# High-part products ahead of low-part products in the first projection behind each norm of a two-block fp32 kernel

## The chip, the cores and the metric

The kernel runs on one core of one Trainium2 chip. The metric is device time in microseconds for one execution. The kernel before took 1255.28 us, the median of three runs (1248.02 to 1257.01).

## The reference, cut to what matters

Two transformer blocks in a row on one sequence of 512 tokens, width 1024, everything in fp32. The first block has two layers; each has an attention mixer and a gated embedding stage behind it ("ple"):

```
for i in range(2):
    h = rms_norm(x, norm_g[i])
    x = x + mixer_i(h)                 # neighbourhood attention, then GQA with rotary
    g = sigmoid(rms_norm(x, ple_norm_g[i]) @ ple_w_gate[i])
    x = x + g * (p[i] @ ple_w_proj[i])
x = rms_norm(x, final_norm_g)
```

The second block is one layer: `h = rms_norm_2(x, norm_g_2)`, a wide input projection `h @ w_in_2`, a sparse attention mixer and a recurrent mixer (RWKV-7) side by side, an output projection, and a last norm. So there are five norms that are followed by a projection: norm0, ple0, norm1, ple1 and norm2.

## The kernel before, in words

**Split products.** TensorE is fed with fp32 numbers that are split in two rounded parts, high and low. A product of activations and weights is made of three: high x high, high activations x low weights, low activations x high weights. `three` (line 498 on) issues them for one k, `tm3` for one tile of 128 tokens and 256 output columns (24 products: 8 values of k times 3), `fm3` for 128 output features and all 512 tokens (24 products of 512 columns). All of them accumulate in one PSUM bank.

**How parts come about.** For weights (a half is 1024 x 256 numbers, in the ring of buffers): SyncE loads them, ScalarE copies the high part (`high`, line 1308), POOL subtracts and leaves the low part in place, in four pieces (`lower`, line 2503). `need3` lets TensorE wait for the fourth piece of a half. For activations behind a norm, in tiles of 128 tokens: VectorE computes the norm and scales a tile (line 1792, semaphore `xn_`), TensorE transposes it (`turn`, two halves of four blocks), VectorE multiplies with the gain out of the bank (`gain_half`, line 1804, or 1801 at norm2), ScalarE copies the high part (`high_half`, line 1313, semaphore `hi_`), and the low part is made by POOL for tiles 0 to 2 (`low_half`, line 2509, semaphore `lo_`) and by VectorE for tile 3 (line 1815, semaphore `lo3_`). A half (hf 0 or 1) holds k = 0 to 3 or 4 to 7.

**Order behind a norm.** Each engine has its own program, written out by hand. TensorE, at the end of the stage ahead, runs `tail`: three tiles, the turn of tile 0, the fourth tile, the turn of tile 1. Then `head`: for tile i the 24 products of block 0 (with the six products of the embedding projection behind them in ple0 and ple1), and behind tiles 0 and 1 the turns of tiles 2 and 3. `head` serves ple0, ple1 and norm1. ScalarE's `head` (line 1319 on) copies the high parts of tile 1, drains tile 0's bank, copies tile 2, then copies the high part of the next weights, drains tile 1, copies tile 3, drains the rest. VectorE's `ple` adds tile 0's result, does the gain of tile 2, adds tile 1's, does the gain of tile 3 and its low parts. POOL makes the low parts of tiles 0 to 2 ahead of those of the next weights.

**norm2** has its own order (lines 758 to 782): all eight transposes, for half 0 of the four tiles and then for half 1; then two `fm3` of 512 tokens with the weights Ckv (banks kvc 0 and 1). POOL makes three of the eight low halves, VectorE five. Behind Ckv come Csel, Cq 0 and others.

The waits sit in front of the products: in `head`, `ready(k)` waits at k = 0 and k = 4 for the low half of the tile, although the first two products of each k read high parts only. At norm0 the same is written out at line 611; that place is not in the diff.

Of the kernel before, what the change touches and what calls it, by code (L numbers as in the profile page):

```python
# [33 lines left out]
P = 128  # L34
# [3 lines left out]
KB = D // P  # L38
# [68 lines left out]
def program(nc, A, out):  # L107
    ctx = ExitStack()
    with ctx:
# [13 lines left out]
        def sem(name):  # L123
            return ctx.enter_context(nc.semaphore(name))
# [41 lines left out]
        for name, src in (("norm0", A["norm_g"][0:1]), ("norm1", A["norm_g"][1:2]),  # L166
# [6 lines left out]
            n = src.shape[1] // P  # L173
# [56 lines left out]
        for part in range(2):  # L230
            for n in range(2):
                w = A["w_out_2"][0][512 * part:512 * part + 512, 512 * n:512 * n + 512]
                load(("CO", part, n), w.rearrange("(k p) n -> p k n", p=P), (4, 512), False)

        def raw_slot(n):
            return ring[:, HALF * (n % NRAW):HALF * (n % NRAW) + HALF]

        def high_slot(n):
            o = HALF * (NRAW + splits.index(n) % NHI)
            return ring[:, o:o + HALF]  # L240
# [18 lines left out]
        def parts(high, low, k):  # L259

            return tuple(rounded(v.rearrange("p (k m) -> p k m", k=k)) for v in (high, low))

        def W3(name):
            n = HI[name]
            k, m = halves[n][1]
            return parts(high_slot(n)[:, 0:k * m], raw_slot(n)[:, 0:k * m], k)
# [25 lines left out]
        def S(name):  # L292

            if name not in made:
                made[name] = sem(name)
            return made[name]
# [17 lines left out]
        def evacuated(eng, key):  # L314

            eng.wait_ge(drained[who[key]], nth[key])
# [128 lines left out]
        def _(pe):  # L445
            def begin(key, consumer, apart=False):

                n = len(order)
                if n >= NBANK:
                    evacuated(pe, order[n - NBANK])  # L450
                order.append(key)
                if not apart:
                    opened.append(key)
                slot[key], who[key] = n % NBANK, consumer
                return bank[slot[key]]
# [3 lines left out]
            def end(ins, key=None):  # L459

                key = key or opened.pop(0)
                J[key] = len(J)
                count[who[key]] += 1
                nth[key] = count[who[key]]
                ins.then_inc(filled, 1)

            def mm(o, l, r, start, stop):
                return nc.tensor.matmul(o, l, r, start=start, stop=stop)  # L468
# [12 lines left out]
            def turn(tag, i):  # L481

                pe.wait_ge(S("xn_" + tag), i + 1)
                for hf in range(2):
                    turn_half(tag, i, hf, xn[:, i % 2, :])

            def need3(name):
                pe.wait_ge(s_wlo, 4 * splits.index(HI[name]) + 4)
# [4 lines left out]
            def three(o, left, right, start, stop):  # L493

                mm(o, left[0], right[0], start, False)
                mm(o, left[0], right[1], False, False)
                return mm(o, left[1], right[0], False, stop)

            def fm3(key, consumer, name, c0, act, ready=None, read=None):

                b = begin(key, consumer)
                w = W3(name)
                for k in range(KB):
                    if ready:
                        ready(k)
                    ins = three(b[:, :], [v[:, k, c0:c0 + P] for v in w], [v[:, k, :] for v in act], k == 0, k == KB - 1)
                    if read and k % 2 and k < KB - 1:
                        ins.then_inc(S(read), 1)
                end(ins)

            def tm3(key, consumer, w, i, c0, act, nk=KB, ready=None, m=256):

                b = begin(key, consumer)
                for k in range(nk):
                    if ready:
                        ready(k)
                    ins = three(b[:, 0:m], [v[:, k, i * P:(i + 1) * P] for v in act], [v[:, k, c0:c0 + m] for v in w],
                                k == 0, k == nk - 1)
                end(ins)
# [6 lines left out]
                jobs(3)  # L526
                turn(tag, 1)

            def head(tag, jobs):

                for i in range(NT):
                    def ready(k):
                        if k % 4 == 0 and i < 3:
                            pe.wait_ge(S("lo_" + tag), 2 * i + k // 4 + 1)
                        elif k % 4 == 0:
                            pe.wait_ge(S("lo3_" + tag), k // 4 + 1)

                    jobs(i, ready)
                    if i < 2:
                        turn(tag, i + 2)  # L540

# [29 lines left out]
            def ple(l, after):  # L571
                act = act3(f"ple{l}")
                pw = parts(pw_hi, pw_lo, 2)
                pT = tuple(rounded(v[:, :, :]) for v in (p_T, p_lo))
                for n in range(4):
                    need3(("PG", l, n))
                    if n == 0:
                        evacuated(pe, ("pT", l, 1))
                        pe.wait_ge(S("pw_low"), l + 1)

                    def jobs(i, ready=None):
                        tm3(("PG", l, n, i), "a", W3(("PG", l, n)), i, 0, act, ready=ready)
                        tm3(("PP", l, n, i), "v", pw, i, 256 * n, pT, nk=2)

                    if n == 0:
                        head(f"ple{l}", jobs)
                    elif n == 3 and after:
                        tail(jobs, after)
                    else:
                        for i in range(NT):  # L590
                            jobs(i)
                    used3(("PG", l, n))
# [5 lines left out]
            b = begin("vec", "a")  # L598
# [5 lines left out]
            act = act3("norm0")  # L604
            for n in AORD:
                need3(("A", n))
                if n == AORD[0]:
                    for i in range(NT):
                        def ready(k):
                            if k % 4 == 0:  # L610
                                pe.wait_ge(S("lo_norm0"), 2 * i + k // 4 + 1)
# [83 lines left out]
            act = act3("norm1")  # L695
            for n in range(10):
                need3(("B", n))
                if n == 0:
                    head("norm1", lambda i, ready: tm3(("B", 0, i), "a", W3(("B", 0)), i, 0, act, ready=ready))
                elif n < 6:  # L700
                    for i in range(NT):
                        tm3(("B", n, i), "a", W3(("B", n)), i, 0, act)
                else:
                    for s in range(2):
                        fm3(("B", n, s), "v", ("B", n), s * P, act)
                used3(("B", n))
            for i in range(NT):
                pe.wait_ge(S("B_rope"), i + 1)
                pe.wait_ge(S("B_rope_k"), i + 1)
                for hf in range(2):  # L710
                    b = begin(("BqT", i, hf), "a")
                    for q in range(4):
                        o = (4 * hf + q) * P
                        ins = nc.tensor.transpose(b[:, q * P:(q + 1) * P], qB[:, i, o:o + P], ident)
                    end(ins)
                b = begin(("BkT", i), "a")
                for g in range(4):
                    ins = nc.tensor.transpose(b[:, g * P:(g + 1) * P], kD[:, i, g * P:(g + 1) * P], ident)
# [44 lines left out]
                    pe.wait_ge(S("xn_norm2"), i + 1)  # L763
                    turn_half("norm2", i, hf, xn4[:, i, :])

            def ready2(k):

                if k % 4 == 0:
                    pe.wait_ge(S("lo_norm2"), (2, 3)[k // 4])
                    pe.wait_ge(S("lo3_norm2"), (2, 5)[k // 4])  # L770

            act2 = act3("norm2")
            need3("Ckv")
            for n in range(2):
                fm3(("kvc", n), "v", "Ckv", n * P, act2, ready2 if n == 0 else None)
            used3("Ckv")

            def tokens(name, key):
# [15 lines left out]
            b = begin("hid", "v", apart=True)  # L794
            for ii in range(16):
                for n, name in enumerate(("W1K", "W1V")):
                    if ii % 8 == 0:
                        need((name, ii // 8))
                    ins = mm(b[64 * n:64 * n + 64, 0:256], fl[:, n, ii * 64:ii * 64 + 64], W((name, ii // 8))[:, ii % 8, :],
                             ii == 0, ii == 15)  # L800
# [13 lines left out]
            for i in range(NT):  # L814
                for name, src in (("qp", q2), ("qr", q2r)):
                    b = begin((name, i), "a")
                    for j in range(4):
                        ins = nc.tensor.transpose(b[:, j * P:(j + 1) * P], src[:, i, j * P:(j + 1) * P], ident)
                    end(ins)
                b = begin(("kz", i), "a")  # L820
                for m in range(4):
                    ins = nc.tensor.transpose(b[:, m * P:(m + 1) * P], kd[:, i, m // 2, (m % 2) * P:(m % 2) * P + P], ident)
                end(ins)
            evacuated(pe, "hid")
            b = begin("hidT", "a")
            for m in range(2):
                ins = nc.tensor.transpose(b[:, m * P:m * P + P], hid_t[:, m * P:m * P + P], ident)
# [28 lines left out]
            b = begin("kcmp", "v")  # L856
            for blk in range(2):
                ins = mm(b[0:64, 0:64], w2[:, 0, blk, :], hid[:, 0, blk * 64:blk * 64 + 64], blk == 0, blk == 1)
            end(ins)
            b = begin("vcmp", "v")  # L860
            for g in range(2):
                for blk in range(2):
                    ins = mm(b[0:32, g * 64:g * 64 + 64], hid[:, 1, blk * 64 + g * 32:blk * 64 + g * 32 + 32],
                             w2[:, 1, blk, :], blk == 0, blk == 1)
# [100 lines left out]
            for j in range(4):  # L965
                bs = [begin((key, j), "a") for key in ("W", "A_")]
# [1726 lines left out]
```

## Time and profile before

| | us |
|---|---|
| median of 3 runs | 1255.28 (1248.02 to 1257.01) |
| the profiled execution, time | 1253.56 |
| the profiled execution, span | 1251.8 |
| TensorE busy | 1152.9 (92%) |
| VectorE busy | 596.9 (48%) |
| ScalarE busy | 509.6 (41%) |
| POOL busy | 450.4 (36%) |
| mean granted TensorE clock | 0.975 of full |

Busy times are sums over the whole span, and the stages differ. The stretches with the changed code are short: ple0 from 313 to 334 us of the span, norm1 from 379 to 397, ple1 from 653 to 675, norm2 from 729 to 753. A matmul row of the timeline shows start and duration; matmuls overlap, so the time that one takes from another's start to its own is shorter than its duration. In brackets stands how long the engine was idle ahead of the row, and what released it. The granted clock is given as a share of 2.4 GHz; its other level is 1.2 GHz, shown as 0.50.

### The profile page before, as it was taken

Reading aid. Unit: us, or ns where it says so; the run is one execution under the profiler, and the core shown is the slowest. Engines: PE = TensorE matmul, PEld = TensorE weight load, DVE = VectorE, ACT = ScalarE, POOL = GpSimd, SP = SyncE. Lnnn points to the kernel's source line nnn. Section 1 sums busy time; section 2 is a strip of 40 time slices with the busy share of each in tenths; the row PEclk is TensorE's granted clock in tenths of the full one; section 3 lists DMA queues with packets and bytes.
Section 4 is the critical chain, followed back from the end, with each engine's and each line's share of the span. In section 5 each row is a group of like instructions: output and inputs, shape, how many; then the busy total and the mean of one; then the engine's idle time right before and its main releaser. Section 6 shows DMA issues by size and latency. Waiting matters only on the chain.

```text
span 1251.8 us, 24943 instructions
## 1 busy us (share of the span) xinstructions
PE 1152.9 (92%) x10379; PEld 967.8 (77%) x10379; DVE 596.9 (48%) x1377; ACT 509.6 (41%) x1038; POOL 450.4 (36%) x391
## 2 busy tenths in 40 slices
PE   3999999999998999899999959988998889999996
PEld 3988887899898998566889949876776777777862
DVE  5000004733637169788245381137845755345546
ACT  4222224942324432888332353155854321133221
POOL 5744475873636445101544345130025460000000
PEclk9999999999999999999999979999999898999998
DMA  7433343332122332000331222431012222100001
GB/s 208 140 102 101 101 119 96 73 88 68 68 68 68 102 101 75 27 2 2 102 102 35 71 98 85 142 112 35 2 35 68 68 67 75 55 28 3 3 2 67
DMA packets 73178, 89.60 MB, mean 72 GB/s; under 512 B 1993, under 2 KB 66634, under 8 KB 72938
## 3 DMA queue, kind: packets, MB, share of 16 engines
q1 hardware_dynamic: 70136, 78.65, 19.5%
q0 software_dynamic: 2416, 8.26, 2.6%
q8 instruction: 82, 1.34, 0.4%
q10 hardware_dynamic: 514, 1.11, 0.4%
q14 instruction: 30, 0.25, 0.1%
HBM read 83.75 MB, written 4.26 MB: 70 GB/s over the span
## 4 chain that ended last, share of the span: by engine, by line
PE 73%; DVE 8%; issue 6%; POOL 5%; ACT 5%; DMA 2%; ACTq 0%; DVEq 0%; POOLq 0%
PE bank L468 68%; POOL ring_parts L2503 3%; PE bank L736 2%; ACT arena L1279 2%; DMA x<-x_kept 1%; DVE stat L1781 1%; PE bank L646 1%; PE bank L904 1%; ACT arena L1395 1%; DVE stat L1782 1%; POOL arena L2625 1%; DVE arena L1804 1%; DVE arena L1792 1%; ACT ring_parts L1308 1%; DVE x L1801 1%
## 5 line engine op out<-in xcount | busy, mean ns | idle before, releaser
L2503 POOL TENSOR_TENSOR ring_parts<-ring,ring_parts 128x512 fp32r<-128x512 f32 (+1 forms) x236 | 306.2, 1330 | 395.1 <-ACT ring_parts L1308 304.7
L468 PE MATMUL bank<-ring_parts,hT_parts 128*128 128x256 f32 x1664 | 329.2, 284 | 12.6 <-POOL arena_parts L2509 7.8
L468 PE MATMUL bank<-hT_parts,ring_parts 128*128 128x512 f32 x896 | 290.1, 402 | 15.7 <-POOL ring_parts L2503 10.0
L468 PEld LDWEIGHTS bank<-ring_parts,hT_parts 128*128 128x128 f32 x1664 | 267.9, 191 | 15.3 <-issue 11.1
L1279 ACT ACTIVATE arena<-bank 128x512 f32<-128x512 f32 (+3 forms) x356 | 166.9, 529 | 272.6 <-PE bank L468 264.2
L468 PE MATMUL bank<-ring_parts,arena_parts 128*128 128x256 f32 x1088 | 255.7, 284 | 3.4 <-POOL hT_parts L2520 3.4
L468 PE MATMUL bank<-arena 64*64 64x64 f32 (+6 forms) x3440 | 218.6, 276 | 9.3 <-ACT arena L1632 2.9
L468 PEld LDWEIGHTS bank<-hT_parts,ring_parts 128*128 128x128 f32 x896 | 173.1, 193 | 58.4 <-POOL ring_parts L2503 8.5
L468 PEld LDWEIGHTS bank<-arena 64*64 64x64 f32 (+2 forms) x3440 | 157.5, 141 | 62.7 <-issue 24.5
L468 PEld LDWEIGHTS bank<-ring_parts,arena_parts 128*128 128x128 f32 x1088 | 188.9, 190 | 4.3 <-POOL hT_parts L2520 3.8
L1308 ACT ACTIVATE ring_parts<-ring 128x2048 fp32r<-128x2048 f32 (+1 forms) x59 | 111.2, 1886 | 79.5 <-PE bank L468 79.4
L468 PE MATMUL bank<-arena_parts,ring_parts 128*128 128x512 f32 x256 | 101.1, 395 | 0.0
L1856 DVE SCALAR_TENSOR_TENSOR arena<-arena,bank 128x512 f32<-128x512 f32 x8 | 5.5, 688 | 172.0 <-ACT arena L1383 172.0
L468 PE MATMUL bank<-x_parts,ring_parts 128*128 128x512 f32 x192 | 78.7, 410 | 0.0
L468 PEld LDWEIGHTS bank<-arena_parts,ring_parts 128*128 128x128 f32 x256 | 48.0, 188 | 10.8
L2520 POOL TENSOR_TENSOR hT_parts<-hT,arena_parts 128x512 fp32r<-128x512 f32 x16 | 20.4, 1281 | 90.7 <-ACT arena_parts L1334 90.6
L2509 POOL TENSOR_TENSOR arena_parts<-arena,hT_parts 128x512 fp32r<-128x512 f32 x26 | 34.4, 1349 | 43.8 <-ACT hT_parts L1313 43.8
L468 PE MATMUL bank<-ring,arena 64*64 64x64 f32 (+3 forms) x512 | 49.2, 303 | 0.8 <-DMA ring<-in_cmp_w_v 0.7
L1509 ACT ACTIVATE arena<-bank,stat 128x512 f32<-128x512 f32 x64 | 43.2, 688 | 13.9 <-PE bank L468 6.7
L2042 DVE TENSOR_REDUCE stat<-bank 128x1 f32<-128x512 f32 x64 | 39.8, 683 | 14.1 <-PE bank L468 14.1
L1923 DVE TENSOR_TENSOR x<-x,bank 128x256 f32<-128x256 f32 x32 | 13.4, 420 | 69.3 <-PE bank L468 69.3
L468 PEld LDWEIGHTS bank<-x_parts,ring_parts 128*128 128x128 f32 x192 | 38.8, 202 | 7.8
(241 smaller groups left out, 1427.1 us busy)
## 6 DMA issues: line engine op xcount, KB each, us to landing
ring<-in_a_w_in SPq DMA_DIRECT2D x16, 1024.0 KB, 5.4
ring<-in_w_in SPq DMA_DIRECT2D x15, 1024.0 KB, 5.4
ring<-in_b_w_in SPq DMA_DIRECT2D x10, 1024.0 KB, 5.1
ring<-in_ple_w_gate SPq DMA_DIRECT2D x8, 1024.0 KB, 4.9
arena<-rpb_rows POOLq DMA_DIRECT2D x16, 256.0 KB, 3.5
ring<-in_a_w_out SPq DMA_DIRECT2D x4, 1024.0 KB, 4.8
ring<-in_b_w_out SPq DMA_DIRECT2D x4, 1024.0 KB, 5.0
ring<-in_w_out SPq DMA_DIRECT2D x4, 1024.0 KB, 5.1
```

What stands on the lines that cost most here:

```text
L468: return nc.tensor.matmul(o, l, r, start=start, stop=stop)
L646: ins = nc.tensor.transpose(b[:, o:o + P], pA[:, u % 8, o:o + P], ident)
L736: ins = nc.tensor.transpose(b[:, k * P:(k + 1) * P], pB[u % 8][:, k * P:(k + 1) * P], ident)
L904: ins = nc.tensor.transpose(b[:, k * P:(k + 1) * P], pN[u % 8][:, k * P:(k + 1) * P], ident)
L1279: return nc.scalar.activation(o, i, ACT.Copy, scale=scale)
L1308: nc.scalar.activation(rounded(high_slot(n)[:, 0:m]), raw_slot(n)[:, 0:m], ACT.Copy).then_inc(s_whi, 1)
L1509: give(nc.scalar.activation(pB[u % 8], b[:, :], ACT.Exp, bias=stat[:, c:c + 1], accum_out=stat[:, c + 8:c + 9]), key)
L1923: give(TT(xs, xs, b[:, 0:w], ALU.add), key)
L2042: nc.vector.tensor_reduce(stat[:, 128 + u % 8:129 + u % 8], b[:, :], X, ALU.max, negate=True)\
L2503: nc.gpsimd.tensor_tensor(rounded(r), r, read_back(high_slot(n)[:, o:o + m // 4]), ALU.subtract)\
L2509: nc.gpsimd.tensor_tensor(rounded(v), v, read_back(tile_of(hTf, tag, i, hf)), ALU.subtract)\
L2520: nc.gpsimd.tensor_tensor(rounded(hT[:, j, :]), hT[:, j, :], read_back(o_high[:, T * j:T * j + T]), ALU.subtract)\
```

## The change

In `head` (ple0, norm1, ple1) a tile's 24 products are issued in another order: first, for k = 0 to 7, the two products with the high part of the activations, which wait only for `hi_`; then, for k = 0 to 7, the product with the low part, which waits for `lo_` or `lo3_` as before. The embedding products come behind as before, through `behind`. At norm2 the two banks are opened together; the 32 products with high parts for both come first, waiting for four and then eight of ScalarE's copies, and the 16 with low parts behind them, bank 0 and then bank 1. The other engines' programs are the same.

```
-            def head(tag, jobs):
+            def head(tag, name, key, act, behind=None):
+                w = W3(name)
                 for i in range(NT):
-                    def ready(k):
+                    ts = slice(i * P, (i + 1) * P)
+                    b = begin(key + (i,), "a")
+                    for k in range(KB):
+                        if k % 4 == 0:
+                            pe.wait_ge(S("hi_" + tag), 2 * i + k // 4 + 1)
+                        for part in w:
+                            mm(b[:, 0:256], act[0][:, k, ts], part[:, k, :], k == 0 and part is w[0], False)
+                    for k in range(KB):
                         if k % 4 == 0 and i < 3:
                             pe.wait_ge(S("lo_" + tag), 2 * i + k // 4 + 1)
                         elif k % 4 == 0:
                             pe.wait_ge(S("lo3_" + tag), k // 4 + 1)
-                    jobs(i, ready)
+                        ins = mm(b[:, 0:256], act[1][:, k, ts], w[0][:, k, :], False, k == KB - 1)
+                    end(ins)
+                    if behind:
+                        behind(i)
                     if i < 2:
                         turn(tag, i + 2)
...
+                    def embed(i):
                         tm3(("PP", l, n, i), "v", pw, i, 256 * n, pT, nk=2)
...
-                        head(f"ple{l}", jobs)
+                        head(f"ple{l}", ("PG", l, 0), ("PG", l, 0), act, embed)
...
-                    head("norm1", lambda i, ready: tm3(("B", 0, i), "a", W3(("B", 0)), i, 0, act, ready=ready))
+                    head("norm1", ("B", 0), ("B", 0), act)
...
-            def ready2(k):
-                if k % 4 == 0:
-                    pe.wait_ge(S("lo_norm2"), (2, 3)[k // 4])
-                    pe.wait_ge(S("lo3_norm2"), (2, 5)[k // 4])
             act2 = act3("norm2")
             need3("Ckv")
+            w = W3("Ckv")
+            bs = [begin(("kvc", n), "v") for n in range(2)]
+            for k in range(KB):
+                if k % 4 == 0:
+                    pe.wait_ge(S("hi_norm2"), k + 4)
+                for n in range(2):
+                    for part in w:
+                        mm(bs[n][:, :], part[:, k, n * P:n * P + P], act2[0][:, k, :], k == 0 and part is w[0], False)
             for n in range(2):
-                fm3(("kvc", n), "v", "Ckv", n * P, act2, ready2 if n == 0 else None)
+                for k in range(KB):
+                    if n == 0 and k % 4 == 0:
+                        pe.wait_ge(S("lo_norm2"), (2, 3)[k // 4])
+                        pe.wait_ge(S("lo3_norm2"), (2, 5)[k // 4])
+                    ins = mm(bs[n][:, :], w[0][:, k, n * P:n * P + P], act2[1][:, k, :], False, k == KB - 1)
+                end(ins)
```

## Rows read from the trace of the kernel before

**Rows 1.** The page, chain that ended last: share of the span by engine

```profile
PE 73%; DVE 8%; issue 6%; POOL 5%; ACT 5%; DMA 2%; ACTq 0%; DVEq 0%; POOLq 0%
```

**Rows 2.** Waits of TensorE over the span: us in total, times, longest us

```profile
PE bank L468 <- POOL arena_parts L2509: 7.8, 5, 2.2
PE bank L468 <- DVE arena_parts L1815: 2.9, 2, 1.9
```

**Rows 3.** Timeline in ple0: start us, us, engine, line, tile, [idle before <- releaser]

```profile
313.63 5.44 POOL L2509 TENSOR_TENSOR arena_parts<-arena,hT_parts 128x512 fp32r<-128x512 f32 x4 [7.81 <-ACT hT_parts L1313]
...
315.05 0.48 PE L468 MATMUL bank<-ring_parts,hT_parts 128*128 128x256 f32 x2 [2.23 <-POOL arena_parts L2509]
...
325.52 5.67 POOL L2503 TENSOR_TENSOR ring_parts<-ring,ring_parts 128x512 fp32r<-128x512 f32 x4
...
328.41 3.34 DVE L1815 TENSOR_TENSOR arena_parts<-arena,hT_parts 128x512 fp32r<-128x512 f32 x2
...
331.80 0.51 PE L468 MATMUL bank<-ring_parts,hT_parts 128*128 128x256 f32 x2
...
332.26 0.40 PE L468 MATMUL bank<-ring_parts,hT_parts 128*128 128x256 f32 x2
...
333.33 0.87 PE L468 MATMUL bank<-arena_parts,arena_parts 128*128 128x256 f32 x6
```

**Rows 4.** Timeline in norm1

```profile
381.25 0.47 PE L468 MATMUL bank<-ring_parts,hT_parts 128*128 128x256 f32 x2 [2.12 <-POOL arena_parts L2509]
...
388.46 2.52 POOL L2509 TENSOR_TENSOR arena_parts<-arena,hT_parts 128x512 fp32r<-128x512 f32 x2 [3.18 <-ACT hT_parts L1313]
...
390.95 6.08 POOL L2503 TENSOR_TENSOR ring_parts<-ring,ring_parts 128x512 fp32r<-128x512 f32 x4
...
397.08 0.51 PE L468 MATMUL bank<-ring_parts,hT_parts 128*128 128x256 f32 x2 [0.86 <-POOL ring_parts L2503]
```

**Rows 5.** Timeline in ple1, tile 3

```profile
668.35 3.31 DVE L1815 TENSOR_TENSOR arena_parts<-arena,hT_parts 128x512 fp32r<-128x512 f32 x2
...
670.13 0.47 PE L468 MATMUL bank<-ring_parts,hT_parts 128*128 128x256 f32 x2 [1.92 <-DVE arena_parts L1815]
...
674.54 0.91 PE L468 MATMUL bank<-arena_parts,arena_parts 128*128 128x256 f32 x6
```

**Rows 6.** Timeline at norm2, both projections of Ckv and the first of Csel

```profile
731.74 3.98 ACT L1313 ACTIVATE hT_parts<-x 128x512 fp32r<-128x512 f32 x4 [2.42 <-DVE x L1801]
...
737.88 4.01 ACT L1313 ACTIVATE hT_parts<-x 128x512 fp32r<-128x512 f32 x4 [2.15 <-DVE x L1801]
...
738.94 0.47 PE L468 MATMUL bank<-hT_parts,ring_parts 128*128 128x512 f32 x1 [4.64 <-DVE x L1801]
...
740.33 4.05 DVE L1815 TENSOR_TENSOR x_parts<-x,hT_parts 128x512 fp32r<-128x512 f32 x3
...
743.77 5.51 POOL L2503 TENSOR_TENSOR ring_parts<-ring,ring_parts 128x512 fp32r<-128x512 f32 x4 [2.77 <-ACT ring_parts L1308]
...
744.53 0.48 PE L468 MATMUL bank<-hT_parts,ring_parts 128*128 128x512 f32 x1 [1.00 <-DVE x_parts L1815]
...
752.79 0.40 PE L468 MATMUL bank<-ring_parts,hT_parts 128*128 128x256 f32 x2
```

**Rows 7.** Stretches: length, TensorE busy (products), granted clock, DMA share, GB/s

```profile
316.00:317.00 1.00, 1.00 (x7) 0.59 1.04 361
...
382.00:383.00 1.00, 1.00 (x11) 1.00 1.09 387
...
671.30:674.70 3.40, 3.40 (x19) 0.52 0.00 0
...
739.50:742.90 3.40, 3.40 (x10) 0.51 0.00 0
```

**Rows 8.** The chain in order of time behind norm2: start us, us, what

```profile
744.53 59.98 PE bank L468 x444
```

**Rows 9.** The page, costliest groups: the weight loads, busy us, mean ns

```profile
L468 PEld LDWEIGHTS bank<-ring_parts,hT_parts 128*128 128x128 f32 x1664 | 267.9, 191 | 15.3 <-issue 11.1
```

More of the change, by code:

```diff
@@ L579, in ple, with jobs @@
                         pe.wait_ge(S("pw_low"), l + 1)
-                    def jobs(i, ready=None):
-                        tm3(("PG", l, n, i), "a", W3(("PG", l, n)), i, 0, act, ready=ready)
+                    def embed(i):
                         tm3(("PP", l, n, i), "v", pw, i, 256 * n, pT, nk=2)
+                    def jobs(i):
+                        tm3(("PG", l, n, i), "a", W3(("PG", l, n)), i, 0, act)
+                        embed(i)
                     if n == 0:
-                        head(f"ple{l}", jobs)
+                        head(f"ple{l}", ("PG", l, 0), ("PG", l, 0), act, embed)
                     elif n == 3 and after:
```

## The prediction

> **What bounds the kernel now.** I read the chain that ended last first: TensorE holds nearly three quarters of it [rows 1], so a microsecond counts only where TensorE waits, or where its work stands on the chain. Then TensorE's waits by releaser [rows 2]: all waits at the norms for low parts of activations come to 7.8 us (POOL, five waits, all in the three heads) and 2.9 us (VectorE, two), beside the 4.64 us ahead of norm2's first product [rows 2, 6]. That is the ceiling of what these waits alone can give. Last I read the timeline of each of the four places, since what a wait is worth depends on what is late next: ple0 [rows 3], norm1 [rows 4], ple1 [rows 5], norm2 [rows 6].
>
> A product of 256 columns takes 0.119 us: nine start between 332.26 and 333.33, the last nine of the twelve behind 331.80, whose first three carry some 0.1 us of start [rows 3]. One of 512 columns takes 0.229 us: 36 between 744.53 and 752.79 [rows 6]. The number of products, weight loads, banks and DMAs stays; no queue but TensorE's is reordered. What moves: per tile, sixteen products with high parts wait only for ScalarE's copies, and the eight with low parts stand behind them.
>
> **ple0.** For tile 0, ScalarE's first copy lets POOL start its low half at 313.63, and TensorE starts at 315.05 after 2.23 us [rows 3]. After the change it starts about 313.7. But that head start is not kept: the turn of tile 2 must wait for VectorE's norm anyway, and tile 3's parts come from a chain of VectorE and ScalarE (gain, copy, low halves from 328.41 to 331.75) which is paced by VectorE's own order and by ScalarE's weight copy ahead of drain 1, not by the products of tiles 0 to 2. So look at tile 3. Before, its k = 4 waits for the second low half until 331.80, and twelve products lie behind: 1.53 us to 333.33. After, the sixteen high products run from 328.4, when the copy is there that VectorE's low half waits for too, to 330.3; four low ones follow, and only four lie behind 331.75: 1.53 - 8 x 0.119 = 0.58 us. The end comes 0.95 us earlier. Late next would be the low parts of the next block's weights, but POOL ends them at 325.52 + 5.67 = 331.19, ahead of the 333.1 at which TensorE, six embedding products later, will want them. **-0.95 us**, passed on in full because TensorE runs without a break to the next norm.
>
> **norm1.** The products of block 0 are not the last thing here. TensorE waits at 397.08 (0.86 us) for the low parts of B 1's weights; POOL makes them from 390.95 to 397.03, straight behind tile 2's low parts (388.46), which wait for ScalarE's copy and that for VectorE's gain [rows 4]; by the code VectorE goes through scales and gains of the four tiles without waiting for a product of this block. Tile 3 ends earlier, by the same eight products, and the wait at 397.08 grows by what was won. **0 us.** Bounds: POOL's row excludes a gain; a loss could come only through the clock, below.
>
> **ple1.** As ple0: low halves end at 671.66 [rows 5], and eight products fewer stand behind. TensorE ran here at half rate from 671.3 to 674.7 [rows 7], tile 3 ended at 674.54 instead of 671.8 + 1.53 = 673.3, so 1.2 us were lost to the clock. If the stretch stays: four products of twice 0.119 us run to 672.75, the six embedding products to about 674.2, and half of the 0.5 us then left is lost too: 674.4 in place of 674.54 + 6 x 0.119 = 675.25, a gain of about 0.9. If it goes: 674.54 - 672.38 = 2.2. I take **-0.9** (the idle ahead only shrinks from 1.92 us to two pieces of about 1 us), 2.2 is the far end.
>
> **norm2.** Today the first product waits for low halves of all four tiles and starts at 738.94, 4.64 us after the last transpose; at k = 4 it waits 1.00 us for VectorE's last low half and restarts at 744.53 with 36 products left, to 752.79 [rows 6]. After: the first sixteen (both banks, both weight parts, k 0 to 3) wait for the fourth copy of ScalarE, 731.74 + 3.98 = 735.72, and run to 735.8 + 16 x 0.229 = 739.5. The next sixteen wait for the eighth, 737.88 + 4.01 = 741.89, plus 0.14 as VectorE's end to TensorE's start shows. Then 32 products are left without a wait (the last low half, 740.33 + 4.05 = 744.38, is long in when they need it, at 746.6): 742.03 + 32 x 0.229 = 749.36. That is 3.4 us earlier. **What is late next:** the low weights of Csel, POOL 743.77 + 5.51 = 749.28, within 0.1 us of this. They start behind ScalarE's weight copy and don't move; if VectorE's copies out of the bank, now earlier, lengthen two of the pieces, they cost up to 1.0 us (the same operation took 6.08 us for four in [rows 4] beside a busy VectorE, 5.51 here). Behind 744.53 the chain is 59.98 us of TensorE alone [rows 8], and the weight copies and loads that follow are released by its products, so they move with it.
>
> **The clock.** The granted clock fell to its lower level, 1.2 of 2.4 GHz, for about 3.4 us in ple1 and at norm2 [rows 7], which costs 1.7 us where all of it is products on the chain. One fell behind the 2.23 us idle of ple0 (without effect, tile 3 had to wait anyway), one behind 1.92 us in ple1, one behind 4.64 us at norm2 (without effect, the wait of 1.00 us came after it); none behind 2.12 us in norm1 [rows 3 to 7]. Norm2 now works for 3.7 us, idles 739.5 to 742.0, and then has 7.3 us of products on the chain. With 2.5 us idle, longer than two that were followed by a fall, I take one stretch there: **3.4 - 1.7 = -1.7 us**. Its ends are 3.4 (none) and 0 (two in a row).
>
> The Trainium skill, "TensorE: Matmul & The Clock Gate", section "HAM oscillation — how this bites in real kernels", speaks against this change: short bursts of products with waits between them fall back to the half clock and start each burst cold, and a loop should keep the work of one tile together. This trace agrees in part: three of the idles named were followed by a fall, one of equal length was not. By the rule norm2 and the longer wait at 397.08 would each start cold, and the gain would be 1.9 us in place of 3.6; rival (c) carries it to the point where it turns the sign.
>
> **Sum.** 0.95 + 0 + 0.9 + 1.7 = 3.6 us. The profiled execution took 1253.56 us, so 1250.0; the median of the runs is 1.72 above it, so **1251.7 us**.
>
> **The rivals.**
> (a) *No new half-rate stretch, and ple1's gone*: 0.95 + 2.2 + 3.4 = 6.6 us, 1248.7. For: idles at the three heads become shorter. Against: the 2.5 us at norm2. 25%.
> (b) *The waits only change their name*: something that doesn't hang on products sets each end, as POOL does in norm1. For: the tie at 749.3 between products and Csel's low parts. Against: behind VectorE's last low half stand twelve products today and four afterwards, and no other engine's work covers the difference. With half of the 1.85 us of the two ple heads and nothing at norm2, 0.9 us: 1254.4. 17%.
> (c) *Slower: the clock.* The gate drops the clock behind the new gaps, where the products are on the chain: tile 3's end in ple0, the run from 397.08 whose idle grows from 0.86 to about 1.8 us, and norm2. A stretch costs 1.7 us. The full-rate gain is 0.95 + 0.9 + 3.4 = 5.3 us, so it decides from the fourth stretch on the chain: one in ple0, one in norm1, two in a row at norm2 give 6.8 - 5.3 = 1.5 us more, 1256.8. For: ple1's fall after 1.92 us. Against: full clock after 2.1 us at norm1. 8%.
> (d) *The reorder itself costs.* In the low run each product has a stationary tile of its own, where before two of three shared one; every product has its weight load either way. No row isolates this. Nearest: a load takes 0.191 us on average [rows 9] beside 0.119 us per product of 256 columns, so above it is 0.07 us on each of the four products behind tile 3's wait, 0.3 us per ple head; at norm2 a product of 0.229 us covers a load. Below nothing, as no load is dropped. I take 0, nearest to the twelve at 0.119 us among which a third already have their own tile; the 0.6 us belongs to the range.
>
> **Chances.** The forecast 50%, (a) 25%, (b) 17%, (c) 8%. Range: from (a) less 2.5 us to (c) plus 0.7, that is 1246 to 1257.5; the runs before alone spread from 1248.0 to 1257.0, so a median of a few is uncertain by 2 to 3 us. A measurement of this kernel tells about 1% from no change, 12.6 us. No case reaches it: under 1242.7 would need nearly twice the largest sum, over 1267.9 more than ten half-rate stretches on the chain. Faster by over 1%: 3%. Within: 95%. Slower: 2%.
>
> **What would show it.** ple0 and ple1: the first product of tile 0 starts with POOL's first low half, no longer behind it; four products stand behind VectorE's second low half of tile 3. norm1: the wait for B 1's low weights grows to about 1.8 us, and the time from POOL's low half of tile 2 to the end of these weights keeps. norm2: first product 3.1 us earlier than now against the transposes, an idle of about 2.5 us, then 32 products without a break, and the wait for Csel's low weights about zero. Wrong if tile 3's copies in the ple heads move with TensorE (then more than 0.95), if Csel's weights end visibly behind the products, or if stretches behind norm2 that this change doesn't touch move by more than the 3.6 us.

## The result, and the profile after

The changed kernel took 1244.79 us, median of ten runs (1236.84 to 1249.58), against 1253.12 us for the kernel before, also ten runs. The ratio is 0.9933, 95% interval 0.9910 to 0.9956: 8.3 us faster, 5.5 to 11.3 by the interval. The forecast of 1251.7 had the sign and missed the size; its range began at 1246.0. A second timing (experiment e9) gave 1246.89 and a ratio of 0.9968, interval 0.9944 to 0.9992. Both together, 21 runs, have a mean of 1245.7 us (a twenty-second, 1312.68 us at a mean clock of 0.844, was in a slow state of the chip and is left out); the 93 runs of the kernel before that were timed beside the experiments have 1252.4. So 6.7 us is the best figure, uncertain by about 2 us, and the first timing lay on the favourable side of it.

The profiled execution of the changed kernel took 1243.96 us with a span of 1242.2, 9.6 us less than before. Where the 9.6 us lie is read by comparing the start of the same instruction in both traces. The first group is the timeline of ple0 (columns as in [rows 3]).

```profile
327.87 1.23 ACT L1333 ACTIVATE hT_parts<-arena 128x512 fp32r<-128x512 f32 x2 [2.13 <-DVE arena L1824]
...
328.65 2.14 PE L468 MATMUL bank<-ring_parts,hT_parts 128*128 128x256 f32 x16 [1.43 <-ACT hT_parts L1333]
330.63 0.63 PE L468 MATMUL bank<-ring_parts,arena_parts 128*128 128x256 f32 x4
331.91 0.75 PE L468 MATMUL bank<-ring_parts,arena_parts 128*128 128x256 f32 x4 [0.65 <-DVE arena_parts L1835]
332.49 0.89 PE L468 MATMUL bank<-arena_parts,arena_parts 128*128 128x256 f32 x6
```

The one wait of tile 3 has become two, 1.43 us for ScalarE's copy and 0.65 us for VectorE's low half, with sixteen high products and four low ones between them. Behind the last wait stand four products in 332.49 - 331.91 = 0.58 us, where [rows 3] had twelve in 1.53.

Norm1, the answer to [rows 4]:

```profile
387.65 2.54 POOL L2529 TENSOR_TENSOR arena_parts<-arena,hT_parts 128x512 fp32r<-128x512 f32 x2 [3.17 <-ACT hT_parts L1333]
...
390.16 6.08 POOL L2523 TENSOR_TENSOR ring_parts<-ring,ring_parts 128x512 fp32r<-128x512 f32 x4
...
396.29 0.50 PE L468 MATMUL bank<-ring_parts,hT_parts 128*128 128x256 f32 x2 [1.79 <-POOL ring_parts L2523]
```

POOL sets the end as before, and the wait has grown from 0.86 to 1.79 us. Everything is 0.8 us earlier, which is what ple0 won; norm1 adds nothing.

Tile 3 of ple1, the answer to [rows 5]:

```profile
666.61 3.31 DVE L1835 TENSOR_TENSOR arena_parts<-arena,hT_parts 128x512 fp32r<-128x512 f32 x2
...
666.72 2.14 PE L468 MATMUL bank<-ring_parts,hT_parts 128*128 128x256 f32 x16 [1.44 <-ACT hT_parts L1333]
668.70 0.63 PE L468 MATMUL bank<-ring_parts,arena_parts 128*128 128x256 f32 x4
669.98 0.74 PE L468 MATMUL bank<-ring_parts,arena_parts 128*128 128x256 f32 x4 [0.65 <-DVE arena_parts L1835]
670.56 0.88 PE L468 MATMUL bank<-arena_parts,arena_parts 128*128 128x256 f32 x6
```

The stretches behind its last wait, and at norm2 the idle and the products behind it (columns as in [rows 7]):

```profile
669.90:673.30 3.40, 3.32 (x28) 1.00 0.18 30
735.70:738.10 2.40, 0.07 (x2) 1.00 0.00 0
738.10:745.50 7.40, 7.40 (x32) 1.00 0.00 0
```

From the start of VectorE's low halves to the start of the embedding products there were 674.54 - 668.35 = 6.19 us; now 670.56 - 666.61 = 3.95. That is 2.2 us, the 0.95 us of eight products and 1.3 us because the half-rate stretch of [rows 7] isn't there: the granted clock is 1.00. At norm2 the clock is full as well. Norm2 itself, answering to [rows 6]:

```profile
731.83 3.88 PE L468 MATMUL bank<-hT_parts,ring_parts 128*128 128x512 f32 x16 [0.90 <-ACT hT_parts L1333]
738.03 3.96 PE L468 MATMUL bank<-hT_parts,ring_parts 128*128 128x512 f32 x16 [2.33 <-ACT hT_parts L1333]
...
739.87 5.58 POOL L2523 TENSOR_TENSOR ring_parts<-ring,ring_parts 128x512 fp32r<-128x512 f32 x4 [2.77 <-ACT ring_parts L1328]
...
741.83 3.79 PE L468 MATMUL bank<-x_parts,ring_parts 128*128 128x512 f32 x16
745.51 0.51 PE L468 MATMUL bank<-ring_parts,hT_parts 128*128 128x256 f32 x2
```

The 32 products run from 738.03 to 745.51 without a break, and Csel's low parts end at 739.87 + 5.58 = 745.45: the tie that the prediction named, and no wait of a product for them.

The differences over the whole span, from the starts of the same instruction:

| TensorE's start of | before | after | after - before | step |
|---|---|---|---|---|
| embedding, tile 3 of ple0 | 333.33 | 332.49 | -0.8 | ple0 |
| B 1 | 397.08 | 396.29 | -0.8 | norm1: nothing |
| embedding, tile 3 of ple1 | 674.54 | 670.56 | -4.0 | ple1 2.2, and 1.0 at 507 |
| Csel | 752.79 | 745.51 | -7.3 | norm2 3.3 |
| the run of products ahead of the reload of x | 1024.70 | 1018.47 | -6.2 | given back 1.1 |
| end of the span | 1251.8 | 1242.2 | -9.6 | 3.2 in that run, 0.2 after |

The step at 507 and the last ones are not in changed code. The stretches show what they are; of the kernel before:

```profile
1024.70:1056.10 31.40, 31.40 (x160) 0.84 0.18 63
498.00:515.00 17.00, 13.73 (x83) 0.90 0.18 62
```

Of the changed kernel, the same work:

```profile
1018.50:1046.70 28.20, 28.20 (x160) 0.94 0.21 69
497.00:514.00 17.00, 12.70 (x85) 1.00 0.18 62
```

The same 160 products took 31.4 us at a mean clock of 0.84 and 28.2 us at 0.94. Of the 9.6 us, 4.2 (1.0 and 3.2) are half-rate stretches that this one execution of before had where no line differs, and 1.1 us between norm2 and 1018 went the other way, in steps of 0.1 to 0.3 us of which no experiment shows the cause. The changed code has 0.8 + 2.2 + 3.3 = 6.3 us.

### The profile page after: what moved, and what is told of

The parts are those of the page before. It is cut to its first block, busy times and chain, and to the rows that moved or that the text cites. A ratio compares the mean times of both kernels' runs of the same rounds, so it can differ in the third digit from the quotient of the medians.

```text
span 1242.2 us, 24944 instructions
## 1 busy us (share of the span) xinstructions
PE 1147.2 (92%) x10379; PEld 963.2 (78%) x10379; DVE 597.9 (48%) x1377; ACT 509.5 (41%) x1038; POOL 451.1 (36%) x391
## 4 chain that ended last, share of the span: by engine, by line
PE 72%; DVE 9%; issue 6%; ACT 5%; POOL 5%; DMA 2%; ACTq 0%; DVEq 0%; POOLq 0%
PE bank L468 67%; POOL ring_parts L2523 3%; PE bank L749 2%; ACT arena L1299 2%; DVE stat L1801 1%; DMA x<-x_kept 1%; PE bank L924 1%; DVE arena L1824 1%; DVE stat L1802 1%; PE bank L659 1%; DVE arena L1812 1%; ACT arena L1415 1%; POOL arena L2645 1%; ACT ring_parts L1328 1%; ACT hT_parts L1333 1%
## 5 line engine op out<-in xcount | busy, mean ns | idle before, releaser
L468 PE MATMUL bank<-ring_parts,hT_parts 128*128 128x256 f32 x1664 | 316.8, 283 | 8.4 <-ACT hT_parts L1333 3.6
L468 PE MATMUL bank<-hT_parts,ring_parts 128*128 128x512 f32 x896 | 285.0, 399 | 13.3 <-POOL ring_parts L2523 10.1
L468 PEld LDWEIGHTS bank<-ring_parts,hT_parts 128*128 128x128 f32 x1664 | 260.1, 190 | 10.6 <-POOL ring_parts L2523 4.0
L468 PE MATMUL bank<-ring_parts,arena_parts 128*128 128x256 f32 x1088 | 242.0, 283 | 4.7 <-POOL hT_parts L2540 3.4
L468 PEld LDWEIGHTS bank<-ring_parts,arena_parts 128*128 128x128 f32 x1088 | 182.1, 189 | 6.5 <-POOL hT_parts L2540 3.8
L468 PE MATMUL bank<-x_parts,ring_parts 128*128 128x512 f32 x192 | 74.9, 403 | 0.0
L478 PE MATMUL bank<-cst,arena 128*128 128x128 f32 x160 | 26.0, 321 | 19.7 <-DVE arena L2096 10.7
```

The source lines that it names most:

```text
L478: ins = nc.tensor.transpose(b[:, q * P:(q + 1) * P], src[:, o:o + P], ident)
```

## The experiments

The theory at their start: the full-rate arithmetic holds (5.3 us), and what goes beyond is the clock. The rival: a wait in one of the places is worth more than the arithmetic says. Ratios are to the kernel before on the same chip, with 95% intervals.

**e1, norm2 alone.** The hunk at norm2, with the old `head`.

> Only norm2 has the new order. Waits theory: 3.4 us less at full clock (2.5 us from the earlier start behind ScalarE's eighth copy, 0.9 us from 32 products in place of 36), so ratio about 0.9973, and the stages ahead of norm2 as before. Clock theory (a half-rate stretch behind the new idle at norm2, as the prediction had it): 1.7 us less, ratio 0.9986. Rival, that most of the measured 8 us comes from norm2: 6 us or more, ratio under 0.9955.

Measured: 1249.85 us, ratio 0.9980 (0.9952 to 1.0009). 2.5 us, between both theories. The interval ends at 6.0 us, so the times alone just fail to exclude the rival's 6; the profile does: it has a half-rate stretch behind the new idle, and from the first transpose of norm2 to Csel this execution took 22.4 us where the kernel before takes 24.1, a gain of 1.7 us (without the stretch the changed kernel takes 20.8, a gain of 3.3).

**e2, ple0 and ple1 alone.** The new `head`, an old copy of it for norm1.

> Only ple0 and ple1 have the new order. Waits theory: eight products of 0.119 us fewer behind VectorE's last low half in each, 1.9 us in all, ratio 0.9985. Clock theory: 1.2 us more in executions in which the half-rate stretch at tile 3 of ple1 goes, 3.1 us in all, ratio 0.9975. Rival, tile 3's copies move with TensorE: 4 us or more, ratio under 0.997, and VectorE's low halves of tile 3 start earlier against its scale of tile 3.

Measured: 1247.60 us, ratio 0.9959 (0.9935 to 0.9982). 5.1 us, more than either theory's number, and 3.1 is inside the interval. The rival's own sign is absent: tile 3's copies hang on VectorE as before (its waits are the 1.44 us and the short one of the changed kernel, and in the changed kernel VectorE's low halves of tile 3 start 8.27 us after its scale of tile 3 in ple0, as in the kernel before). The clock is 1.00 around tile 3 in both heads.

**e3, norm1 alone.**

```
-    head("norm1", lambda i, ready: tm3(("B", 0, i), "a", W3(("B", 0)), i, 0, act, ready=ready))
+    head_new("norm1", ("B", 0), ("B", 0), act)
```

> Only norm1 has the new order. Waits theory: no gain, ratio 1.000; the wait for B 1's low weights grows from 0.86 to about 1.8 us. Clock theory: up to 1.7 us more where the longer idle is followed by a half-rate stretch, ratio 1.001. Rival: a gain of 0.9 us like the other heads, ratio 0.9993.

Measured: 1254.61 us, ratio 1.0014 (0.9991 to 1.0037). No gain, though the rival's 0.9993 is just inside the interval; what speaks against it is the row. In the profile the wait is 1.79 us, and the clock fell behind it. The start of B 1 in e3's timeline:

```profile
400.02 0.51 PE L468 MATMUL bank<-ring_parts,hT_parts 128*128 128x256 f32 x2 [1.79 <-POOL ring_parts L2526]
```

Its stretches behind that, and at tile 3 of ple1:

```profile
400.80:404.20 3.40, 3.40 (x18) 0.51 0.60 209
673.90:677.30 3.40, 3.40 (x18) 0.51 0.02 5
```

So part of rival (c) is real. e4's profile had the same stretch behind norm1, the other four profiles with this code and no filler there (the changed kernel, e6, e8, e9) had none.

**e4, the order everywhere** (in `tm3`). Tests rival (d).

```
...
+                if ready is None and nk == KB:
+                    for k in range(nk):
+                        for part in w:
+                            mm(b[:, 0:m], act[0][:, k, i * P:(i + 1) * P], part[:, k, c0:c0 + m],
+                               k == 0 and part is w[0], False)
+                    for k in range(nk):
+                        ins = mm(b[:, 0:m], act[1][:, k, i * P:(i + 1) * P], w[0][:, k, c0:c0 + m], False, k == nk - 1)
+                    end(ins)
+                    return
...
```

> The change, and in every other projection by tiles (24 products of 256 columns each, some 120 tiles) the same order, high first and low behind, where nothing waits for low parts. Order costs nothing: as the changed kernel, ratio to before 0.993. Rival (d) of the prediction, 0.07 us for each low product with its own tile: 8 x 0.07 x 120 = 67 us more, ratio 1.047; a tenth of that would still show as 1.000.

Measured: 1249.36 us, ratio 0.9982 (0.9959 to 1.0006). Its mean is 3.4 us above that of the changed kernel's 21 runs, not 67. The timeline in B's projections gives the price of the order itself:

```profile
421.99 2.07 PE L468 MATMUL bank<-ring_parts,hT_parts 128*128 128x256 f32 x16
423.89 1.10 PE L468 MATMUL bank<-ring_parts,arena_parts 128*128 128x256 f32 x8
424.83 2.07 PE L468 MATMUL bank<-ring_parts,hT_parts 128*128 128x256 f32 x16
```

Eight low products, each with its own stationary tile, take 424.83 - 423.89 = 0.94 us, 0.118 each, the same as the high ones. Rival (d) falls: its 67 us by the time, and a tenth of them, which the interval still holds, by these rows. About 1.6 us of the excess in this profile is the stretch behind norm1; what the rest is stays open.

**e8, norm2 in the new order with the old waits.**

```
-                    pe.wait_ge(S("hi_norm2"), k + 4)
+                    pe.wait_ge(S("lo_norm2"), (2, 3)[k // 4])
+                    pe.wait_ge(S("lo3_norm2"), (2, 5)[k // 4])
...
```

> The changed kernel, but at norm2 the products in their new order wait for the low halves at k = 0 and k = 4 as before. Waits theory: of norm2's 3.4 us the 2.5 us of the earlier start go and the 0.9 us of four products fewer behind the last wait stay, so 2.5 us slower than the changed kernel, ratio to before 0.995. Rival, the order of the products and not the earlier start gives norm2's gain: as the changed kernel, 0.993.

Measured: 1247.91 us, ratio 0.9947 (0.9929 to 0.9964), the mean 1.9 us above the changed kernel's 21 runs. The earlier start carries most of norm2's gain; the interval doesn't exclude the rival by itself, but the row speaks against it, with 4.04 us of idle ahead of the first product instead of 0.90:

```profile
735.50 9.96 PE L468 MATMUL bank<-hT_parts,ring_parts 128*128 128x512 f32 x32 [4.04 <-POOL x_parts L2527]
```

From the first of the 32 high products to the first low one there are 745.29 - 735.50 = 9.79 us instead of the 7.3 of full rate: the granted clock of this profile is at half from 733.9 to 740.7. So the loss of this one execution, 2.9 us from the first transpose to Csel, is part start and part clock, and cannot be set against the 2.5 us as it stands.

**e12, the heads in the new order, tile 3 with the old waits.** The converse for the clock: the idle is one piece again, though a longer one (3.07 us) than in the kernel before (1.92), since the high products now wait too.

```
-                        if k % 4 == 0:
+                        if k % 4 == 0 and i == 3:
+                            pe.wait_ge(S("lo3_" + tag), k // 4 + 1)
+                        elif k % 4 == 0:
                             pe.wait_ge(S("hi_" + tag), 2 * i + k // 4 + 1)
...
-                        elif k % 4 == 0:
-                            pe.wait_ge(S("lo3_" + tag), k // 4 + 1)
```

> The changed kernel, but tile 3 of each head waits for VectorE's low halves ahead of its high products (k = 0 and k = 4), so that its idle is again one piece of about 2 us and sixteen products stand behind the last wait in place of four. Full-rate arithmetic: 12 x 0.119 = 1.4 us more in each ple head, 2.9 us slower than the changed kernel. Clock theory: the half-rate stretch at tile 3 of ple1, absent from every profile with the new order so far, comes back, 1.2 us more, 4 us in all. Rival, the idle in one piece has no part in the clock: 2.9 us and no stretch there.

Measured: 1251.26 us, ratio 0.9999 (0.9973 to 1.0024): by the ratio all of the change's gain is gone. The mean is 6.0 us above that of its 21 runs and 4.5 us above e9's on the same chip (expected 2.9 or 4); the second, uncertain by 3 us, holds both, so the times don't decide between the theories. The profile does. The half-rate stretch is back in ple1, and ple0 has one at its tile 3 as well. Timeline of tile 3 in ple1:

```profile
671.61 1.19 PE L468 MATMUL bank<-ring_parts,hT_parts 128*128 128x256 f32 x8 [3.07 <-DVE arena_parts L1835]
673.21 2.08 PE L468 MATMUL bank<-ring_parts,hT_parts 128*128 128x256 f32 x8 [0.41 <-DVE arena_parts L1835]
675.08 1.57 PE L468 MATMUL bank<-ring_parts,arena_parts 128*128 128x256 f32 x8
```

Stretches at tile 3 of ple0 and of ple1:

```profile
331.70:335.10 3.40, 3.40 (x19) 0.55 0.02 5
673.10:676.50 3.40, 3.29 (x17) 0.56 0.00 0
```

The second eight high products take 675.08 - 673.21 = 1.87 us where eight take 0.95. So the clock theory holds in this execution, with two such stretches instead of one.

**e5, the kernel before with filler products in the gaps.** A filler multiplies the identity into a bank that the next real product overwrites; three of them took 2.74 us in e6's trace. The comments in this diff and in that of e6 are not in the code.

```
+            def warm(n):
+                m = len(order)
+                if m >= NBANK:
+                    evacuated(pe, order[m - NBANK])
+                for _ in range(n):
+                    mm(bank[m % NBANK][:, :], ident, ap(ident, [(0, 4), (1, P)]), True, True)
...
+                    if i in (0, 3):      # in head, ahead of tiles 0 and 3
+                        warm(2 if i == 0 else 1)
...
+            warm(5)      # ahead of norm2's first product
```

> The kernel before with filler products (128 x 512 fp32 by the identity, into a bank that is overwritten) ahead of the waits of tiles 0 and 3 in the three heads and ahead of norm2's first product, so that TensorE doesn't idle there. Clock theory: the half-rate stretches at ple0, ple1 and norm2 go, of which only ple1's costs time: 1.2 us less, ratio 0.999. Waits theory alone: no change, ratio 1.000. Rival: if fillers outlast the waits, up to 1 us more per place, ratio 1.002.

Measured: 1254.78 us, ratio 1.0005 (0.9986 to 1.0024): no gain. In the profile the clock is 1.00 through both ple heads, and in ple1 the embedding products start 4.89 us after VectorE's low halves instead of 6.19, 1.3 us sooner, as expected: with the idle filled the stretch goes although the order is the old one. But TensorE idled 1.9 us longer in the recurrent part with nothing to wait for that the profile shows, as much as was won and more. Waits of TensorE from 1090 to 1200 in the kernel before (us in total, times, longest):

```profile
PE bank L468 <- issue: 0.8, 3, 0.3
```

And in e5:

```profile
PE bank L468 <- issue: 2.7, 5, 1.0
```

**e7, the changed kernel with fillers in the changed gaps** (1 ahead of tile 3, 2 ahead of B 1, 2 ahead of norm2's k = 4).

> The changed kernel with fillers only in the gaps of the changed code: ahead of tile 3 in the heads (1), ahead of B 1's low weights (2) and of norm2's k = 4 (2). Clock theory: new half-rate stretches are rare there already, at most 1 us less than the changed kernel, ratio to before 0.992. Rival, the change pays for new stretches in most executions: 2 to 3 us less, 0.991 or lower.

Measured: 1245.95 us, ratio 0.9949 (0.9922 to 0.9975), as the changed kernel (its mean is 0.9 us above that of the 21 runs, uncertain by 3). That doesn't show that the new stretches cost little: the profile has none of them, but its waits of TensorE for "issue", for nothing that the profile shows, come to 5.1 us over the span instead of 3.0, which can hide the gain.

**e6 and e11, fillers in seven gaps behind or between the changed places**: the changed kernel and the kernel before.

```
+    warm(2)   # ahead of the last wait of the rotary transposes
+    warm(3)   # ahead of gate_c(0)
+    warm(3)   # ahead of project([6, 7, 0, 1])
+    warm(5)   # ahead of the wait for R_sq
-    project([8, 9, 10, 11])
+    warm(1); project([8, 9]); warm(2); project([10, 11])
+    warm(2)   # ahead of the last output parts
```

> The changed kernel with fillers in the idle stretches behind the changed code (ahead of the rotary transposes' end, of the compressed-attention gates, of four waits in the recurrent projections and of the last output parts). Clock theory: five to seven half-rate stretches of 3.4 us are gone, each worth up to 1.7 us: 5 to 8 us less than the changed kernel, ratio to before about 0.988. Rival, the stretches there lie off the chain: no change against the changed kernel, 0.993. Rival, fillers outlast the waits: slower than the changed kernel by 1 to 4 us.

> The kernel before with only the late fillers. Clock theory: the late half-rate stretches go here too and are independent of the change: 3 to 5 us less than before, ratio 0.997. Rival, part of the changed kernel's gain is that it shifts those stretches: 0 to 1 us.

Measured: e6 1242.86 us (six runs), ratio 0.9917 (0.9893 to 0.9940); e11 1248.52 us, ratio 0.9974 (0.9953 to 0.9996). The fillers give 3.3 us on the kernel before, by the ratio, and 2.5 us on the changed one, by the means; the 5 to 8 us expected of e6 did not come. Both gains are uncertain by 2 us or more. They show that late stretches lie on the path and that most of their cost is there with the change and without it, and not that the two are wholly independent.

**e9, the changed kernel again.**

> The changed kernel once more, unchanged. The parts measured alone came to 2.5 us (norm2), 5.1 us (ple heads) and 1.7 us the other way (norm1) by their ratios. If the whole is their sum and the first ten runs had few half-rate stretches by chance: 5.5 to 6.5 us less than before, ratio about 0.995. If the first timing stands: 8.3 us less, 0.9933.

Measured: 1246.89 us, ratio 0.9968 (0.9944 to 0.9992), 4.0 us less than before, under both expectations. The interval holds the sum of the parts and not the first median's ratio. Its profile has the stretch at norm2 that the forecast counted on, behind 2.32 us of idle. Timeline of e9 at norm2:

```profile
741.26 5.53 PE L468 MATMUL bank<-hT_parts,ring_parts 128*128 128x512 f32 x16 [2.32 <-ACT hT_parts L1333]
746.63 3.81 PE L468 MATMUL bank<-x_parts,ring_parts 128*128 128x512 f32 x16
```

The stretch in it:

```profile
742.10:745.50 3.40, 3.40 (x10) 0.51 0.00 0
```

Sixteen products took 746.63 - 741.26 = 5.37 us instead of 3.8, so here norm2 gave 1.7 us.

**e10, the version that beats both.** e6 with one filler ahead of B 1 and two ahead of norm2's k = 4.

> The changed kernel with the fillers of e6_after_warm_late, one filler ahead of B 1's low weights and two ahead of norm2's k = 4. Clock theory: another 0.5 to 1.5 us less than e6_after_warm_late, ratio to before 0.991, and the smallest spread of all. Rival, the fillers are worth nothing beside the change: 0.994.

Measured: 1238.95 us (six runs), ratio 0.9910 (0.9876 to 0.9944), median 7.9 us below e9's on the same chip. The profiled execution has a span of 1237.2 at a mean clock of 0.988.

## Why the prediction was right or wrong

**ple0, 0.95 us: right in mechanism and size.** Four products in 0.58 us stand behind the last wait, to the hundredth. Missing was the clock. Each of the five profiles with the old waits at tile 3 and no filler there has a half-rate stretch in ple0: two at tile 0, where it costs nothing at the end (the kernel before and e3), three at tile 3 (e1, e11, e12), where it costs about 1.3 us. The prediction calls the stretch at tile 0 without effect, but it made TensorE late, so that the idle ahead of tile 3 was 0.98 and 0.99 us in the two and 1.92 us or more in the three. With the new order and its waits none of eight profiles has a stretch at tile 3.

**norm1, 0: right.** The wait grew to 1.79 us; forecast 1.8. The loss through the clock, held possible, happens in two of six profiles (e3, e4) and costs 1.6 us.

**ple1, 0.9 us: the step that failed first.** "I take -0.9 (the idle ahead only shrinks from 1.92 us to two pieces of about 1 us)". The far end, 2.2 us, is what came, and not by chance: all five profiles with the old waits and no filler there (before, e1, e3, e11, e12) have the half-rate stretch at tile 3, none of eight with the new ones (e7's with a filler), nor e5, where fillers stand in the old idle. Stretches of e1 and e11, then longer ones around tile 3 of e2 and e8:

```profile
672.80:676.20 3.40, 3.40 (x20) 0.59 0.00 0
675.10:678.50 3.40, 3.40 (x17) 0.53 0.00 0
664.00:676.00 12.00, 9.91 (x81) 1.00 0.11 23
664.00:676.00 12.00, 9.91 (x82) 1.00 0.24 72
```

Two idles of 1.4 and 0.65 us with 2.6 us of products between them are not the same as one of 1.9 or 3.1 us. "Only shrinks" treated as equal what the rows hadn't shown to be equal.

**norm2, 1.7 us: arithmetic right, the clock taken for certain.** At full rate it gave 3.3 us for 3.4, with the tie at Csel's low parts. The stretch that I took is there in three of six profiles without a filler (e1, e9, e12), not in the changed kernel's, e4's or e6's. On average the term is about 2.5.

Both clock terms erred in the same direction: 1.3 us in ple1 and 1.6 at norm2 make up the distance from the forecast 3.6 to the 6.3 us, but for 0.2, that the profile shows for the changed code. Rival (a), 6.6 us and 1248.7, is what the profiled execution did; it had 25%, because I asked of each new gap whether a fall can follow it and kept ple1's stretch, whose 1.2 us I had read. That norm2 had no stretch in this execution is luck, as three of six have one. Weighted by how often each stretch stands in the profiles, the parts come to 0.95 + 0.8 (ple0) + 2.2 (ple1) + 2.5 (norm2) - 0.5 (norm1) = 5.9 us, an estimate from these counts, beside the 6.7 of all runs.

**The baseline.** 1248.7 would still have been 4 us above the first median. 1.8 us of it is the three-run median of 1255.28, against 1253.47 for 93 runs. The rest is the spread of the new kernel's median, and it is the clock too: its ten first runs go from 1236.84 us at a mean clock of 0.986 to 1249.58 at 0.977, on a line of 1.4 us per 0.001. I had put this uncertainty at 2 to 3 us and let the range end at 1246, only 2.7 us under rival (a).

**The Trainium skill's rule** on bursts with waits between them ("TensorE: Matmul & The Clock Gate", section "HAM oscillation — how this bites in real kernels") was used in the wrong place. The waits in the page's example are longer than the 2.3 and 1.8 us here, so that it doesn't say of these that each would start cold, as the prediction reads it; in the profiles three of six did at norm2 and two of six at norm1. In the ple heads the rule speaks for the change: the long idle was there before, and the change put products into it.

**The reorder itself, (d): no cost** in e4's rows, 0.118 us per product in either run. Two slips of the prediction didn't matter: the ceiling named first leaves out norm2's own wait of 1.00 us, and the "up to 1.0 us" for slower Csel pieces is more than the 6.08 - 5.51 = 0.57 us that its rows give for four; it measured 5.58. Open stays where e4's excess beyond the stretch at norm1 comes from, and why e2 gained 5.1 us where 3.1 to 4.4 (the latter with ple0's stretch at tile 3) would be accounted for; its interval, 2.3 to 8.2, doesn't need an answer.

## What to carry to other kernels

Where a product reads data of two readinesses, issue what needs only the earlier one first, and count what stands behind the last wait: that count by the price of one product was right to 0.1 us in three places. Filling an idle can count a second time if a half-rate stretch follows that idle in the kernel before: at tile 3 of ple1 it was gone in all eight profiles, while at norm2, where one idle of 2.3 us stayed, three of six had one. Price both, and expect the stretch gone where no long idle is left. A median of a few runs of a kernel with a dozen such stretches is uncertain by 3 us or more, so look at the mean clock beside each time before a difference of that size is believed.

## What the runs showed of the hardware

Added instructions often came with waits far behind them. With fourteen fillers ahead, e5 idled 2.7 us in the recurrent part for issue, that is for nothing that the profile shows, instead of 0.8. One of these idles in e5's timeline:

```profile
1177.65 0.33 PE L468 MATMUL bank<-ring,arena 64*64 64x64 f32 x4 [0.90 <-issue]
```

e6 has one of 1.17 us at the same place in the program. In that part e6 and e11 idle 2.0 us so and e7 2.6, all nine profiles without fillers 0.8 to 1.1. But e10, with the most fillers, has 0.8 again, so their number does not decide it. The last fillers stand over 160 us ahead of it in e6 and over 400 in e5. I read it as the supply of instructions to TensorE; no run tested that. At 1 to 2 us in all it is as large as what the fillers of e5 won.
